# Expert passes: who gives a weight slot back, and where the third and fourth slot stand beside the spreading

## The reference, cut to what matters

```python
y = (silu(xb @ w_gate[e]) * (xb @ w_up[e])) @ w_down[e]
contrib = w_sorted[:, None] * y_disp[dest]
out = zeros((T, D)).at[t_sorted].add(contrib)
```

## Time and profile before

| | us |
|---|---|
| median of 3 runs | 1692.74 |
| lowest, highest | 1691.36, 1692.76 |
| profiled execution | 1691.05 |
| its span | 1688.9 |
| PE busy in the span | 1635.9 (97%) |
| DVE busy | 1010.8 (60%) |
| mean granted clock of PE | 0.979 |

### The profile page before, as it was taken

How to read it: one execution, slowest core, us unless ns; L and a number is a source line. 1 busy time by engine, 2 the same in 40 slices (tenths; PEclk the granted TensorE clock), 3 DMA queues, 4 the chain that set the end, 5 groups by cost and what they waited for, 6 DMA issues and landing times. The chain is left out here.

```text
span 1688.9 us, 26924 instructions
## 1 busy us (share of the span) xinstructions
PE 1635.9 (97%) x11364; PEld 1218.6 (72%) x11364; DVE 1010.8 (60%) x1654; ACT 324.9 (19%) x758; POOL 25.3 (1%) x49
## 2 busy tenths in 40 slices
PE   9999999999988999999999999999999999999998
PEld 8777975443433344398799969994798999699953
DVE  4767445344433433369656677766688566677675
ACT  2332222100000000113232122110233221121100
POOL 0010000000000000000000000000000000000000
PEclk9999999997998999999999999999999999999999
DMA  9323388999999999945322524533534143433540
GB/s 364 153 102 149 150 374 328 400 429 427 427 428 427 427 427 426 425 176 199 150 100 107 203 116 200 200 154 133 212 138 180 71 198 144 183 153 147 200 174 25
DMA packets 30635, 398.03 MB, mean 236 GB/s; under 512 B 3505, under 2 KB 4145, under 8 KB 5810
## 3 DMA queue, kind: packets, MB, share of 16 engines
q1 hardware_dynamic: 29938, 393.66, 57.1%
q10 hardware_dynamic: 576, 2.62, 0.4%
HBM read 395.22 MB, written 1.05 MB: 235 GB/s over the span
## 5 line engine op out<-in xcount | busy, mean ns | idle before, releaser
L1249 PE MATMUL bank<-zone,w 128*128 128x128 f32 (+1 forms) x5632 | 659.9, 279 | 4.7 <-ACT zone L2003 1.7
L1249 PEld LDWEIGHTS bank<-zone,w 128*128 128x128 f32 x5632 | 649.6, 192 | 15.2 <-issue 5.9
L1249 PE MATMUL bank<-zone 128*128 128x128 f32 (+7 forms) x3220 | 478.0, 415 | 11.4 <-DMA zone<-in_w_experts 4.0
L1249 PE MATMUL bank<-w,zone 128*32 128x512 f32 (+2 forms) x1736 | 425.1, 581 | 10.1 <-DMA w<-in_w_experts 8.3
L1249 PEld LDWEIGHTS bank<-zone 128*128 128x128 f32 (+2 forms) x3220 | 308.6, 169 | 169.0 <-issue 139.6
L1249 PEld LDWEIGHTS bank<-w,zone 128*128 128x128 f32 (+1 forms) x1736 | 197.6, 156 | 207.2 <-issue 183.7
L2012 ACT ACTIVATE zone<-bank 128x512 f32<-128x512 f32 (+2 forms) x97 | 52.7, 561 | 420.7 <-PE bank L1249 314.6
L3833 DVE TENSOR_TENSOR w<-w 128x1024 f32<-128x1024 f32 x88 | 103.5, 1218 | 0.0
L3579 ACT ACTIVATE zone<-bank 128x256 f32<-128x256 f32 x88 | 33.7, 385 | 216.9 <-PE bank L1249 216.9
L3841 DVE TENSOR_TENSOR zone<-bank,zone 128x256 f32<-128x256 f32 x88 | 36.3, 422 | 61.7 <-PE bank L1249 34.5
L2814 DVE TENSOR_SCALAR zone<-w 128x1024 f32 x52 | 34.8, 689 | 61.4 <-PE bank L1249 45.4
(11 more groups left out here) (321 smaller groups left out, 978.5 us busy)
## 6 DMA issues: line engine op xcount, KB each, us to landing
w<-in_w_layers SPq DMA_DIRECT2D x66, 2048.0 KB, 8.8
w<-in_w_experts SPq DMA_DIRECT2D x52, 2048.0 KB, 21.5
zone<-in_w_experts SPq DMA_DIRECT2D x42, 2048.0 KB, 23.4
w<-in_w_first SPq DMA_DIRECT2D x15, 2048.0 KB, 8.8
w<-in_w_layers SPq DMA_DIRECT2D x4, 1536.0 KB, 6.3
w<-in_w_layers SPq DMA_DIRECT2D x4, 1024.0 KB, 6.5
w<-in_w_first SPq DMA_DIRECT2D x2, 1024.0 KB, 7.1
zone<-in_w_split SPq DMA_DIRECT2D x2, 1024.0 KB, 8.7
```

The costliest lines, as they stand in the source:

```text
L1249: return eng.matmul(out, lhsT, rhs, start=start, stop=stop, **kw_)
```

## The change

Three things change in the passes, all in order and signalling; no arithmetic changes.

1. In all slots but the last of each part (c or f = 3), the eighth product itself raises `w_used`. The wait for the copy therefore stands ahead of the eighth product. The last slots of a part still use `release`, since their last product closes the bank; in the gate and up parts their wait for the copy stands ahead of the eighth product too.
2. In passes 1 to 6 the further block's rows are gathered right after slot 1, slot 2 is read next with the further block's first products in its middle, and the spreading is made in two halves: one tile after slot 2, one after slot 3 and the second group of extra products. The transposes of the weights follow the second half. In pass 7 the order is the same without the spreading.
3. VectorE follows: `more_in`, copy of slot 2, adds of tile 0, copy of slot 3, adds of tile 1, weights out and placing, weights of the further block, copies of slots 4 to 7. The further block's result is kept in `hid` in place of `sG`.

The hunks on `COUNTS` (how often each bank's semaphores are raised in pass 2, 3 and 4) are left out here; they follow from the order.

```diff
@@ -1211,7 +1211,7 @@
     more_hid = ze.take(EPI * CAP).rearrange("p (f s) -> p f s", f=EPI)
     more_g = ze.take(EPI * CAP)
     more_x = cv("sel")[:, 0:KT * CAP].rearrange("p (k s) -> p k s", k=KT)
-    more_ye = sG
+    more_ye = hid
     dg = sG[:, 0:TT * P].rearrange("p (t s) -> p t s", t=TT)
     squares = zone[:, 3072:5120]
     Xx = Xg.rearrange("p k s -> p (k s)")[:, 0:KT * CAP].rearrange("p (k s) -> p k s", k=KT)
@@ -1774,31 +1774,41 @@
                         for evacuated in banks.taken_up(gp, f"in{c // 2}"):
                             eng.wait_ge(*evacuated)
                     for kk in range(2):
-                        if pass0 and (kind, c, kk) == ("gate", 3, 1):
+                        if (kind, c, kk) == ("gate", 3 if pass0 else 2, 1):
                             more_products(kind, part, 1)
                         for q in range(EPI):
                             r = q * CAP
+                            if (kk, q) == (1, EPI - 1):
+                                more_slot(4 * i + c)
                             ins = mm(bank[r:r + CAP, :], Xg[:, 2 * c + kk, r:r + CAP],
                                      w[:, q * 1024 + kk * FE:q * 1024 + (kk + 1) * FE], c == 0 and kk == 0, c == 3 and kk == 1)
-                            if (c, kk, q) < (3, 1, EPI - 1):
+                            if (kk, q) < (1, EPI - 1):
                                 first_mm(pl, ins)
                     if c == 3:
                         ins.then_inc(*banks.close(pl, kind))
-                    more_slot(4 * i + c)
-                    release(at)
+                    else:
+                        ins.then_inc(*pl.up(sem(f"w_used{at}")))
+                    if c == 3:
+                        release(at)
                     if pass0 and (kind, c) == ("up", 0):
                         weights_T(1)
-                    if not pass0 and (kind, c) == ("gate", 1):
+                    if not pass0 and kind == "gate" and c >= 2:
+                        if c == 3:
+                            more_products(kind, part, 3)
                         if spreading:
-                            spreading.pop()(pl, "prev")
-                        weights_T(0)
+                            spreading[0](pl, "prev", [c - 2])
+                        if c == 3:
+                            weights_T(0)
+                            if spreading:
+                                banks.skip(pl, 3)
+                            spreading.clear()
                     if (kind, c) == ("gate", 2 if pass0 else 1):
                         eng.wait_ge(*pl.need(sem("more_picked"), 1))
                         group(pl, "more_in", [((P, k * CAP, CAP), [(hs[:, t, k * P:(k + 1) * P], Pm_in[:, t, :]) for t in range(TT)])
                                               for k in range(KT)])
                     if c == (2 if pass0 and kind == "gate" else 1):
                         part = opened(pl, f"more_{kind}")
-                    if c % 2 == 1 and not (pass0 and (kind, c) == ("gate", 1)):
+                    if c % 2 == 1 and not (kind == "gate" and (c == 1 or not pass0)):
                         more_products(kind, part, c)
             for evacuated in banks.taken_up(pl, "up"):
                 eng.wait_ge(*evacuated)
@@ -1807,14 +1817,18 @@
             bank = [opened(pl, f"down{n}") for n in range(2)]
             for evacuated in banks.taken_up(pl, "hid"):
                 eng.wait_ge(*evacuated)
-            def down_half(f, half, cols):
+            def down_half(f, half, cols, freeing=None):
                 for q in range(EPI):
                     r = q * CAP
+                    if f < 3 and (half, q) == (1, EPI - 1):
+                        more_slot(8 + f)
                     ins = mm(bank[half][r:r + CAP, :], hidT[:, f, r:r + CAP], cols(q), f == 0, f == 3)
-                    if f < 3 or q < EPI - 1:
+                    if q < EPI - 1 or (f, half) < (3, 0) and half == 0:
                         first_mm(pl, ins)
                 if f == 3:
                     ins.then_inc(*banks.close(pl, f"down{half}"))
+                elif half == 1:
+                    ins.then_inc(*pl.up(sem(f"w_used{freeing}")))
 
             def more_down(part, js):
                 for j in js:
@@ -1835,10 +1849,10 @@
                 rows = slice((2 * t + n) * CAP, (2 * t + n + 1) * CAP)
                 mm(banks.tile(to, f"{pre}{t}{n}"), PmT[rows, t, :], more_ye[rows, :], False, True).then_inc(*banks.close(to, f"{pre}{t}{n}"))
 
-            def spread(to, pre):
+            def spread(to, pre, tiles=range(TT)):
                 for evacuated in banks.taken_up(pl, "weights", "down0", "down1"):
                     eng.wait_ge(*evacuated)
-                for t in range(TT):
+                for t in tiles:
                     for n in range(2):
                         own_rows(t, n, to, pre)
                     for evacuated in banks.taken_up(pl, "more_weights", "more_down"):
@@ -1853,9 +1867,10 @@
                     eng.wait_ge(*pl.need(sem("ld_left"), 16))
                 at, w = slot(pl)
                 for half in range(2):
-                    down_half(f, half, lambda q: (kept, w)[half][:, q * 512:(q + 1) * 512] if split else w[:, q * 1024 + half * 512:q * 1024 + (half + 1) * 512])
-                more_slot(8 + f)
-                release(at)
+                    down_half(f, half, lambda q: (kept, w)[half][:, q * 512:(q + 1) * 512] if split else w[:, q * 1024 + half * 512:q * 1024 + (half + 1) * 512], at)
+                if f == 3:
+                    more_slot(8 + f)
+                    release(at)
                 if f == 0:
                     eng.wait_ge(*pl.need(sem("more_placed"), 1))
                     transposes(pl, "more_weights", [(P, t * P, P, Pm_out[:, t, :], ident) for t in range(TT)])
@@ -2924,12 +2939,14 @@
                 rows_in(pl)
                 more_slot(pl, q, 0)
                 more_slot(pl, q, 1)
-                if i < PASSES - 1:
-                    add_rows(pl, banks, pre="prev")
+                more_in()
+                for t in range(TT):
+                    more_slot(pl, q, 2 + t)
+                    if i < PASSES - 1:
+                        add_rows(pl, banks, [t], "prev")
                 weights_out()
-                more_in()
                 more_weights(pl, e)
-                for n in range(2, 8):
+                for n in range(4, 8):
                     more_slot(pl, q, n)
             if i == 1:
                 left_blocks(pl)
```

More of the change, by code:

```diff
@@ L608 @@
            'filled1': 3,
-           'filled2': 3,
+           'filled2': 2,
            'filled3': 2,
            'filled4': 2,
-           'filled5': 2,
+           'filled5': 3,
            'filled6': 2,
@@ L625 @@
            'taken1': 3,
-           'taken2': 3,
+           'taken2': 2,
            'taken3': 2,
            'taken4': 2,
-           'taken5': 2,
+           'taken5': 3,
            'taken6': 2,
@@ L687 @@
            'w_used9': 2},
- 'pass4': {'filled0': 3,
+ 'pass4': {'filled0': 4,
            'filled1': 3,
-           'filled2': 3,
-           'filled3': 3,
-           'filled4': 3,
+           'filled2': 2,
+           'filled3': 2,
+           'filled4': 2,
            'filled5': 3,
-           'filled6': 2,
-           'filled7': 2,
+           'filled6': 3,
+           'filled7': 3,
            'filter': 1,
@@ L703 @@
            'placed': 1,
-           'taken0': 3,
+           'taken0': 4,
            'taken1': 3,
-           'taken2': 3,
-           'taken3': 3,
-           'taken4': 3,
+           'taken2': 2,
+           'taken3': 2,
+           'taken4': 2,
            'taken5': 3,
-           'taken6': 2,
-           'taken7': 2,
+           'taken6': 3,
+           'taken7': 3,
            'vector_step': 9,
```

## The result

| | before | after |
|---|---|---|
| median of the runs, us | 1692.12 (4 runs, 1691.36 to 1692.76) | 1708.31 (4 runs, 1705.43 to 1710.24) |
| profiled execution, its span | 1691.05, 1688.9 | 1710.24, 1708.0 |
| mean granted clock | 0.979 | 0.989 |

The ratio is 1.0085, 95% interval 1.0071 to 1.0100. The kernel became slower, as forecast, but by about half as much: 1724.0 was predicted, +31.3. The ratio makes it +14.4, the two medians +16.2, and the profiled executions, of which after's is the slowest of its four, +19.2. The granted clock rose where little had been expected of it; over after's four executions it is 0.989 to 0.992.

A forecast was written before the change was run, and what follows sets the result against it. Transfers and a TensorE-VectorE chain with 12.3 us to spare bound the passes closely. Chain growth 45.9, minus 12.3 of transfer waits, minus 2.3 of clock, gave +31.3 us: 1724.0 us, forecast interval 1712 to 1738, range 1698 to 1740.

The forecast's parts named there:

- five of the six stretches stay, a gain of 2.3: Half-clock stretches after the gathering in passes 1 to 6: five of six stay, gaining 2.3 us, between -14 and +14.
- The chain: TensorE and VectorE work over all passes: grows by 45.9 us, of which 12.3 us of transfer waits absorb a part.
- slot 0: First slot of a pass: its copy ends later than the eighth product could start, costing 0.9 us.
- middle: Pass 1, end of slot 1 to end of the gate part: 17.3 us in place of 15.7, cost 1.6.
- slot 4's copy: First slot of the up part: its copy ends 3.9 us after the spreading, costing 2.8 us, the largest term.
- slot 8: First slot of the down part: its copy already ends after its products, so a lone product adds 0.75 us.
- pass 0: First expert pass: three or four lone products behind late copies cost 2.8 us, between 0 and 3.4.
- The lone product at 0.86: A slot's eighth product, starting alone after a late copy, delays the next full-width product by 0.86 us, bounds 0 and 0.86.
- The dip at 330 to 340: Transfer rate in pass 1: the third slot is read some 6 us sooner, so this dip, 1.6 us, goes.
- Passes 6 us further apart: Sign to look for: pass starts about 6 us further apart than before.
- rival 1: Lone products cost little, or most low-clock stretches vanish: 1695 to 1712 us; chance 0.15.
- Rivals 2 and 3: Transfers stay in charge, 1690.8 us, chance 0.09; or all dips vanish, faster by over 0.2%, 1688.0 us, chance 0.04.

The follow-up runs named there:

- e12: e2 with the spreading whole, behind slot 3, instead of split; 1692.65 us, ratio to before 0.9996.
- e10: The kernel before with the first extra products moved behind the first half of slot 2; 1694.44 us, ratio to before 1.0005.
- e11: The kernel before with the gathering moved ahead of the spreading, right behind slot 1; 1694.30 us, ratio to before 1.0005.
- e1: The kernel before, order unchanged, with only the new signalling: a slot's eighth product waits for the copy and gives the slot back; 1699.28 us, ratio 1.0035.
- e8: e4 with the new signalling in all slots but 0, 4, 6, 8 and 9; 1692.42 us, ratio to before 0.9997.
- e9: e8 with the old signalling in slots 2 and 3 as well, leaving the new one in slots 1, 5, 7 and 10; ratio to before 0.9989.
- e2: The kernel before with only the new order of the change, keeping the old signalling; 1691.69 us, ratio to before 0.9997.
- e4: e2 with VectorE's copies of slots 4 and 5 ahead of the second tile's additions; 1692.04 us, ratio to before 0.9990.
- e5: The kernel before with three full products put into the 0.6 us wait behind the gathering; 1693.05 us, ratio to before 1.0001.
- e7: e1 with the wait for the copy ahead of the slot's last four products instead of the eighth; 1703.83 us, ratio to before 1.0064.

## Why the prediction was half right

**The failed step is the clock.** Of a total of +31.3, the term "five of the six stretches stay, a gain of 2.3" measured 15.4: half-clock time fell from 64.8 to 34.1 us. Over all executions it is about the same: 0.990 in after against 0.979 is some 18 us of work. The forecast's end of -14 nearly reached it, but the value taken was wrong twice.
- It took the stretches for a result of the transposes, the thin products and the 0.6 us wait, which stay close together. In the profiles they come mostly where the spreading stands next to the gathering, and the change parts these (e12 against e10 and e11). The gathering's share went from 27.3 us (before) to 13.7 in two passes, and one of 6.8 in pass 0 came new. A gathering of after, pass 4, with what stands around it:

```profile
488.00:500.00 12.00, 12.00 (x99) 7.43 (x101) 2.75 (x7) 1.14 (x4) 0.00 (x0) 1.00 1.00 425
```

- It priced only these six and put the rest at nothing, without a reason. This is the larger part. The other 37.5 us of half clock in before (64.8 - 27.3) are six stretches behind idle times of 2.1 to 3.1 us; in after 13.7 us are left of them. One of the six (3.4 us) stood behind the wait of 3.1 us for a transfer, and went with it. Two, the largest among them, stood behind waits for the product of gate and up (idle 2.55 and 2.21 us; 2.27 and 1.92 in after, with no fall behind them):

```profile
400.50:414.00 13.50, 13.50 (x63) 6.20 (x65) 4.89 (x11) 1.78 (x4) 0.00 (x0) 0.50 1.00 424
```

That the shorter waits explain it is not shown: a wait of 2.09 us in after is followed by a fall in pass 4 and by none in pass 5, its five waits of 1.60 us by none, one of 1.99 by 3.4 us. The same share fell in e1 (37.5 to 10.2), where the stretches at the gathering grew by nearly as much (27.3 to 51.2, one of pass 0 included). So some 24 of after's 31 us at half clock are of this kind, and their cause stays open for the most part; 7 net are the gathering's, where e1, with the old order, has 31 more than after. Both belong to the sum, because a kernel that keeps the old order pays at the gathering what it saves elsewhere, as e1 does.

**The chain held.** Forecast 45.9, measured 46.7 as the remainder 19.1 + 12.3 + 15.3; that the two lie within 1 us is partly luck, since the remainder is not that exact. Piece by piece, against the rows: slot 0, 0.9 (from its first products at 318.78 to the gathering at 323.36 is 4.58 us; before, from 313.72 to the spreading at 317.46, 3.74: 0.84); middle 17.3 (17.7); slot 4's copy 3.9 behind the spreading (3.89); slot 8, 0.75 (0.98). Slot 0 of pass 1 starts 5.1 us later than before, 3.4 of them for half clock in pass 0, so pass 0 is 1.7 (2.8). Slots 6 and 9 and pass 7 were not read singly. Slot 0's products began with the row at 313.72 itself, not a step ahead of it as the prediction says, which changes nothing. The lone product at 0.86, which no row of before showed, measured 0.83 to 0.98 in e8 and after, and 11.9 us in 14 of them in e9. Full-width work behind it was the right ground to choose it, and it need not follow at once: slot 0 is followed by slot 1, on quarters, and pays ahead of the gathering.

**The waits for transfers** went from 12.3 to 0, as forecast. As forecast too: the queue below 427 GB/s in the last passes, and waits of 1.6 us in most passes and 2.0 in one for slot 4's eighth product (forecast 2.0). The wait at slot 3 is hardly seen as idle (0.1 us in pass 1); it hides in the row, as in e8. The layers are equally long, 967.2 us in both. The third issue of the row that began at 316.7 came 16.6 us behind the first, and comes 12.0 behind it: 4.6 sooner, where 6 was forecast. The dip at 330 to 340 (334 and 380 GB/s before) did not go, it moved and grew. In pass 0 the load issued at 286.1 before is issued at 289.7 in after, so there the slot came back later and not sooner (after runs at half clock there for 6.8 us); around the wait of slot 4 in pass 1 the queue runs dry too. TensorE waits for no transfer behind either. After, busy time by windows:

```profile
285.00:290.00 5.00, 5.00 (x34) 1.56 (x30) 2.39 (x11) 0.60 (x1) 0.00 (x0) 0.64 0.50 213
345.00:350.00 5.00, 3.40 (x34) 0.87 (x32) 2.78 (x9) 0.00 (x0) 0.00 (x0) 1.00 0.60 206
```

**Passes 6 us further apart** held in the first two passes alone. The small products of the down part behind slot 8 mark a pass. Before, passes 1 to 4:

```profile
352.25 2.04 PE L1249 MATMUL bank<-const,zone 128*128 128x32 f32 x16
406.18 3.46 PE L1249 MATMUL bank<-const,zone 128*128 128x32 f32 x16
458.57 1.87 PE L1249 MATMUL bank<-const,zone 128*128 128x32 f32 x16
522.49 2.75 PE L1249 MATMUL bank<-const,zone 128*128 128x32 f32 x16
```

After, the same:

```profile
361.41 1.87 PE L1249 MATMUL bank<-const,zone 128*128 128x32 f32 x16
420.97 1.87 PE L1249 MATMUL bank<-const,zone 128*128 128x32 f32 x16
475.49 1.87 PE L1249 MATMUL bank<-const,zone 128*128 128x32 f32 x16
533.76 2.88 PE L1249 MATMUL bank<-const,zone 128*128 128x32 f32 x16
```

The lag is 9.2, 14.8, 16.9 and 11.3 us. The first is near the 2.8 of pass 0 and 6.8 of pass 1, and pass 2 adds 5.6, but pass 3 adds only 2.1. In pass 4 after wins 5.6 back: before waited there for transfers, 3.1 us once, and ran at half clock behind it. The waits and falls of before were not spread evenly, so the forecast's even steps could only be right in sum.

**The rivals.** The result lies in rival 1's interval (1695 to 1712), and for its second reason, vanished stretches; but rival 1 priced only the six at the gathering, and most of what vanished stood elsewhere, so its number is right by luck. Its first reason, cheap lone products, is refuted by the rows of e8 against e2 (0.97 and 0.83 us) and by e9. Rivals 2 and 3, transfers in charge and faster, would have needed a chain that grew by less than 10 us: e2, e4 and e9 are such kernels or near it, and stand at -0.03 to -0.11%. Little more was to be won behind the seventh slice, since in e9 the queue moves 426 to 428 GB/s from the eighth to the sixteenth:

```profile
GB/s 363 156 100 149 150 373 319 428 426 427 428 427 427 427 427 427 420 166 200 150 100 107 206 113 200 200 155 133 212 138 181 69 197 145 183 154 146 200 174 25
```

The change meant to give slots back early to a queue that was already full, and paid for it on the engine that was second in line.

## What to carry to other kernels

Give a buffer back by its own last product only where everything else that the hand-back waits for is done by then; if a wait breaks up a group that runs side by side, the late product costs a whole turn (0.86 us here), paid at the next work that needs the full width, and the trace may show it as a longer row and not as idle time. When transfers and a chain of engines bound a stretch almost equally, count the slack (12.3 us here) before trading one for the other: savings on the chain came out as waiting, and losses beyond the slack lengthened the run. Price the clock from all its half-clock stretches, not from those at the changed place alone, and compare it over all executions, not in one profile. Keeping groups that load TensorE little apart from each other is worth a try; the profiles speak for it.

## What the runs showed of the hardware

- The granted clock fell to 1.2 GHz with no pause of TensorE shown, at the gathering (0.51 in e5's row above), and filling the only wait left 5 of 7 such stretches (6 of 7 before). With spreading and gathering next to each other it fell in 40 of 49 passes of the profiles, apart in 13 of 49.
- The same place is not sure to fall: before falls in 6 of 7 passes, e1 in 7, after in 2. Each profile is one execution, and the mean clock of one kernel ranges as far as 0.976 to 0.990 over twelve executions (e2), which is 47 us at half clock.
- Away from the gathering, half clock took 10.2 us in e1 and 41.0 in e7, whose waits for the same copies are 0.86 us longer (17.5 us in 16 waits in place of 6.2 in four). The chain did not grow with these waits (16.7 against 18.3), but the clock cost 13.7 us more.
- In a group of four float32 products on four column quarters, one product alone (two records) and four (eight records) take 1.05 and 1.06 us in the rows of e1 and e7. Behind a late product the other quarters go ahead with the next slot (four records at 320.67 in after), and the late quarter ends 0.86 us behind them.
